# A two-layer decoder step: the expert loops in another order, a latent projection whose norm is split between its weights and its results, and loads moved into the loop's tail

## What is computed

```python
def rms_norm(x, g):
    return x * lax.rsqrt(jnp.mean(x * x, axis=-1, keepdims=True) + 1e-6) * g

def mla_project(h, pos, w_dqkv, norm_q, norm_kv, w_uq):     # h = rms_norm(x, norm_attn[1])
    a = h @ w_dqkv                                          # (rows, 1024) @ (1024, 384 + 256 + 32)
    cq = rms_norm(a[..., :384], norm_q)
    c = rms_norm(a[..., 384:640], norm_kv)
    kr = apply_rope(a[..., 640:], pos)
    q = cq @ w_uq
    ...

def expert_block(xb, e):                                    # up to 64 rows of one expert in the kernel
    hb = jax.nn.silu(xb @ w_gate[e]) * (xb @ w_up[e])       # (64, 1024) @ (1024, 256), twice
    return hb @ w_down[e]                                   # (64, 256) @ (256, 1024)
# a row's two results, each times its gate, are added to the row
```

## Time and profile before

| | us |
|---|---|
| median of 3 runs | 2519.2 (2514.76 to 2519.45) |
| the profiled execution's own time | 2523.59 |
| its span, first to last instruction | 2521.9 |
| mean granted TensorE clock | 0.941 of full speed |

### The profile page before, as it was taken

The page is one execution under the profiler, slowest core; times in us unless marked ns, Lnnn a source line. Parts: engine busy times, 40 slices in busy tenths (PEclk is TensorE's granted clock), DMA queues, the critical chain, the costliest instruction groups (busy, mean ns, idle before and its releaser), DMA issues. The chain is left out here.

```text
span 2521.9 us, 28167 instructions
## 1 busy us (share of the span) xinstructions
PE 2209.3 (88%) x10116; PEld 1060.7 (42%) x10116; DVE 832.7 (33%) x2194; ACT 637.5 (25%) x1431; POOL 223.5 (9%) x359
## 2 busy tenths in 40 slices
PE   6999989989888888859999999987998888888876
PEld 3444445563233333335645545554555333333322
DVE  2444455541211101134325555532553221110114
ACT  2444441111111111124435555532111111111112
POOL 0010101111011101100000000040000101110110
PEclk9999998989998998979999999998998989898998
DMA  6000017258999999774330101053527999999986
GB/s 222 18 17 9 5 49 266 99 234 348 419 419 419 417 415 414 316 276 136 95 79 13 26 13 26 1 140 106 204 84 287 385 419 418 419 415 415 413 352 264
DMA packets 141101, 572.07 MB, mean 227 GB/s; under 512 B 35554, under 2 KB 56354, under 8 KB 88626
## 3 DMA queue, kind: packets, MB, share of 16 engines
q1 hardware_dynamic: 88530, 484.00, 48.3%
q10 hardware_dynamic: 30464, 45.96, 5.1%
q0 software_dynamic: 21968, 40.29, 4.3%
HBM read 532.47 MB, written 73.37 MB: 240 GB/s over the span
## 5 line engine op out<-in xcount | busy, mean ns | idle before, releaser
L1545 PE MATMUL m_ps_gu<-ring,m_xT 128*64 128x512 f32 x2080 | 547.1, 674 | 145.0 <-issue 139.0
L1545 PEld LDWEIGHTS m_ps_gu<-ring,m_xT 128*64 128x64 f32 x2080 | 168.3, 153 | 441.8 <-issue 427.0
L1554 PE MATMUL m_ps_y<-ring,m_hT 128*64 128x512 f32 x1040 | 237.5, 598 | 16.9 <-DVE m_hT L1406 16.4
L1400 DVE TENSOR_TENSOR m_h<-m_act,m_ps_gu 128x256 f32<-128x256 f32 x64 | 27.0, 421 | 660.7 <-ACT m_act L1133 660.7
L1444 PE MATMUL m_ps_y<-w_o,oT_all 128*128 128x512 f32 x512 | 234.3, 608 | 3.6 <-PEq L174 3.6
L1133 ACT ACTIVATE m_act<-m_ps_gu 128x256 f32<-128x256 f32 x64 | 24.6, 384 | 675.0 <-PE m_ps_gu L1545 675.0
L584 PE MATMUL a_ps_q<-a_w,a_hT 128*128 128x512 f32 x384 | 180.5, 612 | 4.9 <-DMA a_w<-swa_w_qkv 3.7
L2239 PE MATMUL h_ps_s<-h_kT,h_qT 96*128 96x512 f32 (+3 forms) x384 | 145.5, 488 | 0.9 <-DVE h_kT L2155 0.9
L1056 POOL DMA_INDIRECT expert_rows<-m_y,m_rows_i x64 | 64.5, 1007 | 895.9 <-DVE m_y L1410 868.4
L1444 PEld LDWEIGHTS m_ps_y<-w_o,oT_all 128*128 128x128 f32 x512 | 96.1, 195 | 109.1 <-issue 109.1
L1554 PEld LDWEIGHTS m_ps_y<-ring,m_hT 128*64 128x64 f32 x1040 | 68.9, 136 | 142.1 <-issue 111.4
(11 more groups left out here) (417 smaller groups left out, 2654.4 us busy)
## 6 DMA issues: line engine op xcount, KB each, us to landing
ring<-moe_w_gate SPq DMA_DIRECT2D x130, 1024.0 KB, 21.0
ring<-moe_w_up SPq DMA_DIRECT2D x130, 1024.0 KB, 25.4
ring<-moe_w_down SPq DMA_DIRECT2D x130, 1024.0 KB, 19.5
x_ffn<-misc ACTq DMA_DIRECT2D x18, 512.0 KB, 5.1
normed<-m_y ACTq DMA_DIRECT2D x18, 512.0 KB, 3.5
p_yr<-expert_rows SPq DMA_DIRECT2D x8, 1024.0 KB, 6.6
ring<-expert_rows SPq DMA_DIRECT2D x8, 1024.0 KB, 13.8
a_w<-swa_w_qkv SPq DMA_DIRECT2D x12, 512.0 KB, 11.0
```

What stands on the lines that cost most here:

```text
L1545: ins = eng.matmul(gu_now[r], xT_now[:, i, r], w[:, slot, s, 0:2, DE * i:DE * i + DE], start=i == 0, stop=i == KC - 1)
L1554: ins = eng.matmul(ps_y[r, n, :], hT[:, i, r], w[:, slot, s, 2, D * i + 512 * n:D * i + 512 * n + 512], start=i == 0, stop=i == 1)
```

## The change

1. In the loop, PE does `h_turn` and `down_pair` of pair k - 1 before `gate_up` of pair k; ACT and DVE have the same order.
2. The last pair's gate and up weights come in halves, with a semaphore of their own for the second, and PE starts on the first.
3. At the loop's start, four of the seven transfers of L968 wait until the first gather has landed, and the last `keep_busy` has 44 transposes.
4. An overflow pair's down weights have their own semaphore, and come last. All register loads of SP go ahead of its six transfers.
5. At the end of layer 0's loop SP loads `w` as soon as the down multiplication of pair 30 is done, DVE multiplies it there by the norm's vector (eight instructions of 128x672), and SP issues the expert rows of the first two tiles when the last scatter has landed. The vector comes as 8 numbers for each partition.
6. In the projection PE turns x itself; the root factor is applied where ACT copies the results to `a` (one instruction more for the sample tile). The root of tile i is made behind the addition of tile i + 1. The first prompt tile's first product goes ahead of the sample tile's `c_turn`.

```diff
@@ tail_phase, SP
+            def load_halves(k):
+                for half in range(2):
+                    at = slice(KC * DE // 2 * half, KC * DE // 2 * (half + 1))
+                    for s in range(2):
+                        for n, src in enumerate((wg, wu)):
+                            eng.dma_start(w[:, k % RING, s, n, at], src[2 * k + s][:, at]).then_inc((late_in if half else gu_in[k % RING]), 16)
...
-            load_parts(1, ((0, 0), (0, 1), (1, 0), (0, 2)))
+            load_parts(1, ((0, 0), (0, 1), (1, 0)))
+            eng.wait_ge(xg_in[0], 16)
+            load_parts(1, ((0, 2),))
             load_parts(2, ((1, 0), (1, 1), (1, 2)))
             for k in range(RING, EPAIRS):
                 eng.wait_ge(gu_made, k - RING + 1)
-                load_gate_up(k)
+                if k < EPAIRS - 1:
+                    load_gate_up(k)
+                else:
+                    load_halves(k)
                 eng.wait_ge(y_made, k - RING + 1)
                 load_down(k)
             if layer == 0:
                 eng.wait_ge(space["caches_out"], 32)
-            eng.wait_ge(y_made, EPAIRS - RING + 1)
+                eng.wait_ge(y_made, EPAIRS - 1)
+                for k in range(0, KC, 4):
+                    eng.dma_start(space["next"]["w"][:, k:k + 4, :],
+                                  io["mla_w_dqkv"][0].rearrange("(p c) n -> p c n", c=KC)[:, k:k + 4, :]).then_inc(early["w_in"], 16)
+            else:
+                eng.wait_ge(y_made, EPAIRS - RING + 1)
             each_overflow(eng, overflow)
+            if layer == 0:
+                for u in range(2):
+                    eng.wait_ge(y_out[u], 16 * (EPAIRS // 2))
...
+                eng.dma_start(space["next"]["yr"][0:NS, 0], ys[PT, 0:NS]).then_inc(early["yr_in"][0], 16)
+                eng.dma_start(space["next"]["yr"][:, 1], ys[0]).then_inc(early["yr_in"][1], 16)
@@ tail_phase, DVE
             for k in range(EPAIRS):
-                gated(k)
                 if k:
                     down_out(k - 1)
+                gated(k)
                 behind(k)
             down_out(EPAIRS - 1)
+            if layer == 0:
+                n = space["next"]
+                eng.wait_ge(last_in, 80)
+                eng.wait_ge(early["w_in"], 32)
+                for k in range(KC):
+                    eng.tensor_scalar(n["w"][:, k, :], n["w"][:, k, :], n["gain"][:, k:k + 1], None, ALU.mult).then_inc(early["w_done"], 1)
@@ tail_phase, PE
-            keep_busy(64)
+            keep_busy(44)
...
             for k in range(EPAIRS):
+                if k:
+                    h_turn(k - 1)
+                    down_pair(k - 1)
                 eng.wait_ge(xT_done, k + 1)
                 eng.wait_ge(gu_in[k % RING], 64 * (k // RING) + 64)
                 if k >= 2:
                     eng.wait_ge(h_done, k - 1)
                 for i in range(KC):
+                    if k == EPAIRS - 1 and i == KC // 2:
+                        eng.wait_ge(late_in, 64)
                     ins = gate_up(xT[:, k % 2], ps_gu[:, k % 2], k % RING, i)
-                    if i == 3 and k:
-                        h_turn(k - 1)
                 ins.then_inc(gu_made, 1)
                 if k + 1 < EPAIRS:
                     turn(k + 1)
-                if k:
-                    down_pair(k - 1)
@@ mla_projection_phase, SP
-            load_expert_rows(0)
-            load_expert_rows(1)
-            for k in range(0, KC, 4):
-                eng.dma_start(w[:, k:k + 4, :], io["mla_w_dqkv"][0].rearrange("(p c) n -> p c n", c=KC)[:, k:k + 4, :]).then_inc(w_in, 16)
             for k in range(3):
                 eng.dma_start(wq[:, k, :], io["mla_w_uq"][0].rearrange("(c p) n -> p c n", p=P)[:, k, :]).then_inc(wq_in, 16)
@@ mla_projection_phase, ACT
                 if ORDER[i] == PT:
...
+                    eng.wait_ge(rstd_done, i + 1)
+                    eng.wait_ge(a_done, 4)
+                    eng.activation(a[0:NS, :], a[0:NS, :], ACT.Copy, scale=rstd[0:NS, 0:1]).then_inc(a_done, 1)
                 else:
-                    eng.copy(a[:, 0:512], ps_a[:, 0, :]).then_inc(a_done, 1)
-                    eng.copy(a[:, 512:DQ], ps_a[:, 1, 0:KB]).then_inc(a_done, 1)
+                    eng.wait_ge(rstd_done, i + 1)
+                    eng.activation(a[:, 0:512], ps_a[:, 0, :], ACT.Copy, scale=rstd[:, 0:1]).then_inc(a_done, 1)
+                    eng.activation(a[:, 512:DQ], ps_a[:, 1, 0:KB], ACT.Copy, scale=rstd[:, 0:1]).then_inc(a_done, 1)
@@ mla_projection_phase, DVE
             def add(i):
...
-                ch.link(eng.reciprocal(rstd[:, 0:1], rms[:, 0:1]))
-                wait_if(eng, hT_made, i)
-                eng.scalar_tensor_tensor(out=h[:], in0=x[:, sl, :], scalar=rstd[:, 0:1],
-                                         in1=gain, op0=ALU.mult, op1=ALU.mult).then_inc(h_done, 1)
+                eng.reciprocal(rstd[:, 0:1], rms[:, 0:1]).then_inc(rstd_done, 1)
@@ mla_projection_phase, PE
-                eng.wait_ge(h_done, i + 1)
+                eng.wait_ge(x2_done, i + 1)
...
-                    ins = eng.transpose(ps_t[:, P * k:P * k + P], h[:, k::KC], ident[:])
+                    ins = eng.transpose(ps_t[:, P * k:P * k + P], x[:, i % 2, k::KC], ident[:])
```

90 lines of the change are left out of this document (55 added, 35 removed).

## The result

| | before | changed |
|---|---|---|
| median | 2519.3 us (2514.8 to 2521.5, 4 runs) | 2496.1 us (2494.3 to 2498.3, 4 runs) |
| profiled execution, its span | 2523.6, 2521.9 | 2498.3, 2496.4 |
| mean granted clock | 0.941 | 0.945 |

The ratio is 0.9912, with a 95% interval of 0.9896 to 0.9928: 23.2 us are won, where 40.7 were forecast. The changed kernel is faster, and the time lies 1 us above the range of the prediction.

The account below looks back on a forecast made before the run. TensorE was taken to bound the projection, full DMA engines the expert loops. Starts 14 + ends 19.2 - overflow 1 - seam 1.5 + projection 10.0 = 40.7 us, so the median goes from 2519.2 to 2478.5, range 2466 to 2495.

Parts of the forecast that it names:

- The loops' start: Start of each expert loop: an earlier first gather and down product win 7 of 8.4 us idle, 14 in all.
- The loop's order: Inside the loops: TensorE's new wait between turned h and down product is hidden by the transfers, cost 0.
- The loops' end: Last pair of each loop: 10.1 us left from gate_up's second half to the copy; gains 11.0 and 8.2.
- The overflow pair: Behind the second loop: its weights follow without a gap, 3.6 us of turning and copying ahead; cost 1 us.
- The seam: First loop's last copy to projection: weights land 2 us after the copy, scaling takes 4; cost 1.5 us (0 to 6).
- The projection's start: Projection's first instruction to first prompt tile's turned cq: four terms together win 10.0 us, bounds 7 and 13.
- (a): Loops' starts: gathers are slow by themselves, not by the queue; each start gives 3 instead of 7, 2486; chance 0.14.
- (c): Expert loops: TensorE becomes the bound through the new wait and the half clock; about 2530, slower than before; chance 0.03.
- (b): Loops and seam: uneven queues decide; starts give 5 each, last down weights 3 us late, w another 3; 2491.5; chance 0.13.

Follow-up runs that it names:

- e2: Changed kernel with pair 31's gate and up weights in whole transfers, gate multiplied first, then up: 2496.5 us (0.9903).
- e1: Changed kernel with layer 1's x rows and norm_final for the final phase issued by SP behind the overflow pair's down weights: 2496.0 us (0.9906).
- e7: Changed kernel with the new order of the loop undone on TensorE, ACT and DVE: 2516.8 us (0.9988).
- e8: Changed kernel with held-back loads, halves and order of the loop all undone: 2520.5 us (1.0002).
- e6: Changed kernel with the halves undone, pair 31's gate and up weights whole and all waited for: 2497.1 us (0.9901).
- e9: Changed kernel with ACT's five projection loads issued earlier and six unread transposes ahead of layer 0's last h_turn: 2497.6 us (0.9907).
- e13: e12 with a separate semaphore for the vector scaling w, so DVE waits for it and w alone; broadcasts issued first: 2489.9 us (0.9873).
- e12: Changed kernel plus e1, e2, e3, e9, overflow gate weights and product before up's, its rows turned earlier, norm_final's broadcast issued first: 2490.9 us (0.9874).
- e3: Changed kernel with 28 unread transposes in the projection ahead of the first prompt tile's c_turn: 2497.2 us (0.9908).
- e4: Changed kernel with all seven weight transfers, not four, held back until the first gather has landed: 2505.5 us (0.9942).
- e5: Changed kernel without the held-back loads and with 64 transposes in the last keep_busy: 2499.3 us (0.9907).

## Why the prediction was wrong

Where the gains would come was right, and the sum was too high: by 12 us in four terms that the profiles can place, by 17.5 in the medians. The largest failed step is the overflow pair's (4). Where the profiles differ by less than the 3.6 and 2.5 us by which one loop varies, the split between terms is a reading of single executions, not shown by times.

1. **The loops' start.** "All in all 7 of the 8.4 us in each loop": 7.8 and 7.2 less idle time. The size was right and half of the way to it was not. The step that failed is that the queue would be dry at 556: it was dry at 561. Of these 5 us 2.9 are the later start of the loop in this execution; counted from the gather's issue the queue was dry after 6 us where 3.7 were forecast, since I took three gathers (4 us) off the backlog that still stood in it. So the gather was 2.2 us sooner instead of 4.5, `gate_up` of pair 0 took 8.79 us, 1.5 more than two halves at the full clock, and the refill went out 19.0 us behind the gather's issue, not 14.7. The first gap closed all the same, since the four held-back transfers, issued from 562 on, were themselves still under way until just ahead of the refill. The second gap closed by the order, as forecast. Undone, the order gives 5.4 us of idle time back, 4.2 of them in the second gap (6.8 in all against 1.4), and holding back gives 2.4.
2. **The loop's order** costs nothing, as forecast: the wait for hT grew by 0.9 us a pair (0.6 forecast) and is hidden.
3. **The loops' end** was to give 11.0 and 8.2. By difference, with the idle time taken off, loop 1 gave 16.8 - 7.8 = 9.0 and loop 2 13.4 - 7.2 = 6.2. The 10.1 us from the second half to the copy came exactly in loop 2; in loop 1 it was 11.8, since down ran at the lower clock (5.35 us for 3.65), which is 1.7 of the 2.0 missing there, and TensorE waited for neither half. The 2.0 of loop 2 may be the halves themselves, an estimate by e2's windows: their packets move 22 bytes a nanosecond where whole ones move 26, and 4.2 MB lose 1.7 us. The halves had been costed at nothing.
4. **The overflow pair** was to cost 1 us and cost 6.2: this is the largest error. 4.0 are wait (5.59 for 1.59), 1.9 are clock (9.03 for 7.09). The step "they [...] now follow without a gap, with 3.6 us of turning and copying ahead of their use" counted no bytes: 6.3 MB behind the last gate and up weights are 15 us, the work in front of them 13. e1 shows 1.8 us of the wait to be the rows of the final phase. With the old order (e7, e8) the pair doesn't wait and the stage takes 22, and without the halves (e6) it takes 25.2: a gain ahead of a wait for bytes is lost to it, and 8.2 us had been booked there.
5. **The seam** was to cost 1.5 and cost 2.4 (1.5 to 2.7 in the five profiles with the same loop). I had the condition in the bracket, "0 if `w` is early, 6 if the slowest engine brings it last". e7 and e8 show how far that goes, 8 us. By e9 and e13 it is landing, not issue, that decides: the last of ACT's five loads is last of all, and `w` was there 1.4 to 2.4 us ahead of it in the changed kernel, e7, e9 and e12. The rule of the Trainium skill, SBUF — State Buffer, § SBUF: two separate sides, on VectorE's two-port instructions and GpSimd's descriptors wasn't tested: the scatter had been issued 2.0 us before the scaling began (1071.45 and 1073.41). In e6 the two overlapped by 0.5 us, with the scatter first; it landed 4.0 us behind its issue (4.1 in the changed kernel), and the scaling took 4.15 us instead of 3.92.
6. **The projection's start** gave the forecast 10.0, and not by errors that cancel: the first turn came 6.5 us sooner (6.4 forecast with the first two terms) and the first product 7.9 (7.8 with the third). That it fits to the tenth is luck, since the same stretch gave 8.5 to 10.6 in the other profiles. What failed is the sentence "from the turned cq of the first prompt tile on all is as before": of the product behind it 2.1 us, and with its neighbours 2.8, were lost to the clock, which fell in a wait that had grown from 1.57 to 3.55 us. That the clock is the reason is shown by e3, in the profile; the loss came in five of ten profiles, those in which the clock had not fallen ahead of the wait.

Of the rivals (a) is refuted by e4, (c) by e7 and the windows. (b) came nearest with 2491.5, but for the most part by another sum: its starts give 5 each, where 7.8 and 7.2 less idle time were measured. What it says of landings holds at the seam and in e12. The Trainium skill's rule that a bulk load runs at the pace of its slowest engine (DMA: Bandwidth & Descriptors, § iDMA fabric — 4 AXI ports for 8 engines, asymmetric across TPBs) agrees with e12, where the load's last packet ended 10 us behind the window in which the share fell under a half. But (b) put the loss at the last down weights, where no wait showed (0.77 and 0.54 us for hT only).

What stays open: how much of the overflow's remaining wait of 3.8 us is the slowest engine and how much the mean, as no view parts the engines; why the start of the program varies by 7.6 us; why the clock falls now ahead of the wait in the projection and now in it; and where the last 2.3 us of the medians are.

## What to carry to other kernels

Where a stage ends on bytes, count them up to the next wait that needs them, before booking a gain ahead of it: what was won there came back at the next load. A load into a reused slot is only as early as the instruction that frees the slot, so the worth of "early loads" can lie wholly in the order of another engine's work, as in e8. And a wait in a busy stretch can cost most of its length again: here waits of 2.9 to 3.6 us were followed by 1.7 to 2.9 us lost to the lower clock. Where such a loss is missing in one profile, look ahead of the wait before calling it chance.

## What was not expected of the hardware

- The granted clock fell from 1.00 to 0.50 (1.2 of 2.4 GHz) in a wait of 3.55 us in a stretch that was otherwise busy, was 0.50 from 1108.1 to 1114.9, and the product there took 9.15 instead of 7.03 us. In e1 it was 0.50 from 1090.7 to 1094.1 instead, in the product ahead, and 1.00 behind a wait of 1.76 us.
- Half rows of weights in packets of 4096 bytes took 185 ns each while whole ones of 8192 took 315; the throughput was 355 GB/s with them and 407 without, though the engines were busy 0.94 of the time.
- A gather of 512 KB was in use 4.1 to 4.2 us behind its issue with the engines idle (e4), and was in use 7.1 to 9.8 us behind its issue with weights queued ahead of it (9.8 in e5).
- A load of 4.6 MB behind a long full stretch thinned out slowly (e12): the DMA share was 0.49 in 2424 to 2428, then 0.31 and 0.18, and the last packet ended at about 2438.2. A scatter issued 5 us ahead of that end landed with it, in 5.7 us instead of 2.5.
